# A two-layer hybrid trunk in one kernel: chunk inverses computed in pairs over four quadrants, SSD outputs and output tiles issued earlier

## The chip, the cores and the metric

One core of one Trainium2 chip. The metric is the device time of one execution in microseconds, the median of several runs.

## The reference, cut to what matters

Two layers over 384 tokens of 1024 features (128 of a context, 256 latent), in fp32. A layer does

```
h = rmsnorm(x) * (1 + scale) + shift
u = h @ w_in                       # attention 768, RWKV 896, SSD 772 columns
o = [attention | RWKV-7 | Mamba-2 SSD]      # 512 | 256 | 256 features
x = x + gate1 * (o @ w_out)
x = x + gate2 * moe(rmsnorm(x) ...)         # 16 experts, top 2 within the top group
```

RWKV-7 is a delta-rule scan in both directions: per step `S = S*w - (S kk) b' + v k'`, `y = S r`. In the kernel it is computed by chunks of 64 tokens, in which the delta rule is the inverse of a unit triangular 64x64 matrix `I - N` for each of 4 heads, each chunk and both directions.

## The kernel before, in words

All engines run hand-ordered instruction streams; semaphores tie them. Activations are kept transposed (feature by token, W = 385 columns with a gap between context and latent tokens). PSUM's eight banks are given out in turn by a plan (`psum_plan`, L225): the n-th group of matmuls takes bank n mod 8 and waits until the reader of group n - 8 (VectorE "v" or ScalarE "a") has read it (`open_bank`, L722). Weights come as items of 1 MB through SP's DMA queue, strictly in the order of their use (`homes_of`, L431); each item has a home, one of 5 ring slots, 3 places in `u`, 5 in the arena, one in `sq`, one in `hT`. From attention to the fourth output tile only two ring slots (`KEPT`) serve the stream; the others are lent as work space. Between the parts stand "fills": a twelfth of the next layers' modulation vectors, 2 items each (`fill`, L1076).

A layer runs: norm, input projection, attention, then the recurrence stage (`RW_ORDER`, from `rw_order`, L153), then `mixer_ends` (L1440), `out_projection` (L1485), norm, MoE.

The recurrence stage. Six batches (`RW_BATCHES`: a tile of two chunks in one direction; the two chunks stand on partitions 0-63 and 64-127) are inverted in three pairs (0,1), (2,3), (4,5). Each of the ten `RW_STEPS` is done for the first batch, then for the second, followed by SSD work (`SSD_BESIDE`) and, in the second and third pair, by the chunk recurrences whose inverses are done (values, carry, solve, state, output). On TensorE (`inverse_step`, L1280) "matrices" makes the products g4 and the base N (nd); "power1" to "power4" square N and its transpose (p) and build up the inverse of the 16x16 diagonal blocks (t: `inv += P^T' inv`); "transpose" gives `invT`; "cross0", "merge0", "cross1", "merge1" join the blocks to 32 and 64. A group `eight` (L1227) is 4 heads by two halves:

```
for j in range(4):
    for q in HALVES:
        last = mm(bank[q, at + 64 * j:at + 64 * j + 64], lhsT[q, j, :], rhs[q, j, :])
```

so rows 0-63 of the array feed columns 0-63, rows 64-127 feed columns 64-127. ScalarE (L1907) copies p, tT; VectorE (L2357) masks g4, nd, cross and adds t, t5, tt in place to `inv` or `invT`.

`mixer_ends`: RWKV's group mean (gnm), SSD's output of token tile 0 (`ssd_output`, L1461), the group variance (gnv), the fill "ssd", SSD's tiles 1 and 2, the fill "gate", and the mean square of the gated SSD output (yms), from which ScalarE and VectorE make features 6 and 7 of `o`. `out_projection` makes x's 8 feature tiles n for the tokens 0 to 256 (half 0), then for the rest. `OUT_AHEAD` = 2 tiles begin with features 0 to 5 (attention and RWKV) and get 6 and 7 when `mix_ready` is up. The weight items of tiles 0-1 and 2-3 take the two ring slots after the gate's, those of 4-5 and 6-7 further ring slots.

GpSimd (L938) issues DMAs only: cache and state outputs, row scatters and gathers of the MoE.

Of the kernel before, what the change touches and what calls it, by code (L numbers as in the profile page):

```python
# [13 lines left out]
P = 128  # L14
D = 1024
KT = D // P
TILES = 3
# [90 lines left out]
RW_STEPS = ["matrices", "power1", "power2", "power3", "power4", "transpose", "cross0", "merge0", "cross1", "merge1"]  # L108
# [19 lines left out]
def recurrence(q):  # L128
# [9 lines left out]
SSD_BESIDE = {  # L138
    (0, "matrices"): [("ssd_columns", 0), ("ssd_rows", 0)],
    (0, "power1"): [("ssd_rows", 1)], (0, "power2"): [("ssd_rows", 2)],  # L140
    (0, "power3"): [("ssd_rows", 3)], (0, "power4"): [("ssd_carry", 0)],
    (0, "transpose"): [("ssd_tokens", 0)], (0, "cross0"): [("fill", "rw"), ("ssd_tokens", 1)], (0, "merge0"): [("ssd_tokens", 2)],
    (0, "cross1"): [("ssd_args", 0)], (0, "merge1"): [("ssd_args", 1)],
    (2, "matrices"): [("ssd_args", 2)], (2, "power1"): [("ssd_args", 3)],
    (2, "power2"): [("ssd_decays", 0), ("ssd_args", 4)], (2, "power3"): [("ssd_args", 5)],
    (2, "power4"): [("ssd_args", 6)], (2, "transpose"): [("ssd_args", 7)], (2, "cross0"): [("ssd_decays", 1)],
    (2, "merge0"): [("ssd_queries", 0)], (2, "cross1"): [("ssd_queries", 1)], (2, "merge1"): [("ssd_queries", 2)],
    (4, "matrices"): [("fill", "rw2"), ("ssd_queries", 3)], (4, "power1"): [("ssd_values", 0)], (4, "power2"): [("ssd_values", 1)],
    (4, "power3"): [("ssd_values", 2)], (4, "transpose"): [("ssd_scores", 0)], (4, "cross0"): [("ssd_scores", 1)],
    (4, "merge0"): [("ssd_scores", 2)]}  # L150
# [64 lines left out]
OUT_AHEAD, SSD_FEATURES = 2, 6  # L215
# [9 lines left out]
def psum_plan():  # L225
# [11 lines left out]
    for l in range(DEPTH):  # L237
# [44 lines left out]
        for step, b in RW_ORDER:  # L282
            if step == "matrices":
                for half in range(2):
                    g("v", "g4", l, b, half)
                for half in range(2):
                    g("v", "nd", l, b, half)
            elif step[:5] == "power":
                k = int(step[-1])
                if k > 1:  # L290
                    g("v", "t", l, b, k)
                if k < 4:
                    g("a", "p", l, b, k)
            elif step == "transpose":
                g("a", "tT", l, b)
            elif step[:5] == "cross":
                g("v", "cross", l, b, int(step[-1]))
            elif step == "merge0":
                g("v", "t", l, b, 5)
                g("v", "tt", l, b, 0)  # L300
            elif step == "merge1":
                g("v", "tt", l, b, 1)
            elif step == "factors":
# [28 lines left out]
            elif step == "ssd_states":  # L332
                g("v", "hst", l)
        for i in range(2):
            g("v", "gnm", l, i)
        for grp in range(2):
            g("v", "ys", l, 0, grp)
# [3 lines left out]
        for t in range(1, TILES):  # L341
            for grp in range(2):
                g("v", "ys", l, t, grp)
# [87 lines left out]
def homes_of(stream, plan):  # L431
# [6 lines left out]
    for n, (where, _) in enumerate(stream):  # L438
# [63 lines left out]
def program(nc, a):  # L502
# [6 lines left out]
    with ctx:  # L509
# [221 lines left out]

        def filled(eng, *key):
# [70 lines left out]
        state_ready = sem("state_ready")  # L803
        matrices_ready = sem("matrices_ready")
        gn_in_ready = sem("gn_in_ready")
# [63 lines left out]
        def _(sp):  # L869
            sp.dma_start(cond[:, :], a["cond"][:, :]).then_inc(cond_loaded, 16)  # L870

            def home_free(l, n):

                name, i = HOMES[home[n]]
                if item_before[n] is not None:
# [62 lines left out]
        def _(pool):  # L938
# [80 lines left out]
        def _(pe):  # L1019
# [206 lines left out]

            def eight(bank, at, lhsT, rhs):  # L1227
# [6 lines left out]
            def rwkv_step(l, step, b):  # L1234
                if step == "fill":
                    fill(l, b)
                elif step in RW_STEPS:
# [42 lines left out]
            def inverse_step(l, step, b):  # L1280
                t, d = RW_BATCHES[b]
                s = b % 2
                pw, pwT = power[s][:, 0, :, :], power[s][:, 1, :, :]
                if step == "matrices":
                    if b == 0:
                        pe.wait_ge(factors_ready, 2 * l + 2)
                    banks_ = [open_bank(pe, "g4", l, b, half) for half in range(2)]
                    for i in range(2):
                        for k in range(2):
                            for c, q in enumerate(HALVES):  # L1290
                                c0 = COL[t] + CHUNK * c
                                for half, p in enumerate(HALVES):
                                    at = (2 * i + k) * P
                                    last = mm(banks_[half][q, at:at + P], kb[p, k, d, i, c0:c0 + CHUNK],
                                              ar[p, d, i, :, c0:c0 + CHUNK])
                                    if i and k and c:
                                        last.then_inc(psum_filled, 1)
                    banks_ = [open_bank(pe, "nd", l, b, half) for half in range(2)]
                    for i in range(2):
                        for c, q in enumerate(HALVES):  # L1300
                            c0 = COL[t] + CHUNK * c
                            for half, p in enumerate(HALVES):
                                last = mm(banks_[half][q, i * 64:i * 64 + 64], ar[p, d, i, 0, c0:c0 + CHUNK],
                                          kb[p, 1, d, i, c0:c0 + CHUNK])
                                if i and c:
                                    last.then_inc(psum_filled, 1)
                elif step[:5] == "power":

                    k = int(step[-1])
                    if k == 1:  # L1310

                        pe.wait_ge(matrices_ready, len(RW_BATCHES) * l + b + 1)
                    else:
                        bank = open_bank(pe, "t", l, b, k)
                        taken(pe, "p", l, b, k - 1)
                        if k > 2:
                            taken(pe, "t", l, b, k - 1)
                        eight(bank, 0, pwT, inv[s]).then_inc(psum_filled, 1)
                    if k < 4:
                        bank = open_bank(pe, "p", l, b, k)  # L1320
                        last = eight(bank, 256, pw, pwT)
                        if k < 3:
                            last = eight(bank, 0, pwT, pw)
                        last.then_inc(psum_filled, 1)
                elif step == "transpose":
                    bank = open_bank(pe, "tT", l, b)
                    taken(pe, "t", l, b, 4)
                    for j in range(4):
                        for q in HALVES:
                            last = mm(bank[q, 64 * j:64 * j + 64], inv[s][q, j, :], C("ident64", q))  # L1330
                    last.then_inc(psum_filled, 1)
                elif step[:5] == "cross":

                    k = int(step[-1])
                    bank = open_bank(pe, "cross", l, b, k)
                    if k:
                        taken(pe, "t", l, b, 5)
                    eight(bank, 0, g4[b][:, :, 2, :], inv[s]).then_inc(psum_filled, 1)
                elif step[:5] == "merge":
                    k = int(step[-1])  # L1340
                    if k == 0:
                        bank = open_bank(pe, "t", l, b, 5)
                        taken(pe, "cross", l, b, 0)
                        taken(pe, "tT", l, b)
                        eight(bank, 0, invT[b], cross[s]).then_inc(psum_filled, 1)
                    bank = open_bank(pe, "tt", l, b, k)
                    taken(pe, "cross", l, b, k)
                    if k:
                        taken(pe, "tt", l, b, 0)
                    eight(bank, 0, cross[s], invT[b]).then_inc(psum_filled, 1)  # L1350

            def recurrence_step(l, step, q):
# [17 lines left out]
                if step == "values":  # L1370
                    bank = open_bank(pe, "rv", l, q)
                    taken(pe, "tt", l, batches[1], 1)
# [19 lines left out]
                elif step == "solve":  # L1392
                    bank = open_bank(pe, "x", l, q)
                    taken(pe, "rv", l, q)
# [45 lines left out]
            def mixer_ends(l):  # L1440

                for i in range(2):
# [3 lines left out]
                ssd_output(l, 0)  # L1446
# [5 lines left out]
                ssd_output(l, 1)  # L1452
                ssd_output(l, 2)
                fill(l, "gate")
                bank = open_bank(pe, "yms", l)
                pe.wait_ge(gated_sq_ready, l + 1)
                for i in range(2):
                    last = mm(bank[:, 0:W], C("ones"), sq[:, 2 + i, :], i == 0, i == 1)
                last.then_inc(psum_filled, 1)
# [35 lines left out]

# [1490 lines left out]
```

## Time and profile before

| | us |
|---|---|
| median of 3 runs (1082.76 to 1089.31) | 1085.03 |
| profiled execution, its own time | 1091.34 |
| its span | 1089.5 |
| TensorE busy, share of the span | 969.5, 89% |
| VectorE / ScalarE busy | 483.1 / 275.3 |
| mean granted TensorE clock | 0.967 |

The profile is of one execution. Busy time of TensorE contains pipelining: a matmul's record runs on while the next has begun. fp32 matmuls are two instructions each. Weight loads have records of their own (PEld). All matmuls come from the helper at L1035, so a group is told by its operands: the inversions are `sb_u` with `sb_u`, `sb_tmp`, `sb_arena` or `sb_consts`, products and bases `sb_hT` with `sb_sq`, the output projection `sb_o` with `sb_ring`. A clock of 1.0 is 2.4 GHz, 0.5 is 1.2 GHz.

### The profile page before, as it was taken

How to read it: one execution, taken by the hardware profiler on the slowest of the kernel's cores; microseconds unless marked ns; L12 is line 12 of the kernel's file. 1: busy time of each engine (PE TensorE's matmuls, PEld its weight loads, DVE VectorE, ACT ScalarE, POOL GpSimd, SP SyncE). 2: the span in 40 equal slices, each digit the busy share in tenths (PEclk: the TensorE clock that was granted, in tenths of full speed). 3: DMA queues.
4: the chain of work that ended last, by engine and by line, in shares of the span. 5: the costliest groups of instructions: out<-in, count | busy, mean ns of one | idle time of the engine just before them, and what ended most of it. 6: DMA issues, size and time to landing. Idle time of an engine off the chain costs nothing. (4 is left out here: it accounts for less than half of the span.)

```text
span 1089.5 us, 25653 instructions
## 1 busy us (share of the span) xinstructions
PE 969.5 (89%) x11169; PEld 703.1 (65%) x11169; DVE 483.1 (44%) x1373; ACT 275.3 (25%) x628; POOL 51.4 (5%) x79
## 2 busy tenths in 40 slices
PE   6799998988879989978999998999987998996596
PEld 4455566778758875645845555778866977663265
DVE  1362388567732433113456066747853351311125
ACT  2330317332111601210242123643210241111000
POOL 0000000000000020012000000000000002001120
PEclk9899999999989999989999999999998999999899
DMA  9769633422268779999732204332038649999992
GB/s 382 290 159 273 160 106 127 157 81 86 82 247 343 301 226 399 373 359 406 312 118 78 78 5 155 118 118 81 9 122 338 263 173 329 375 360 356 374 387 60
DMA packets 43448, 238.75 MB, mean 219 GB/s; under 512 B 5120, under 2 KB 8192, under 8 KB 19904
## 3 DMA queue, kind: packets, MB, share of 16 engines
q1 hardware_dynamic: 29904, 196.37, 47.0%
q0 software_dynamic: 9584, 34.35, 10.5%
q10 hardware_dynamic: 3840, 6.29, 1.8%
q8 instruction: 93, 1.52, 0.6%
q14 instruction: 27, 0.22, 0.1%
HBM read 210.25 MB, written 26.74 MB: 218 GB/s over the span
## 5 line engine op out<-in xcount | busy, mean ns | idle before, releaser
L1035 PE MATMUL bank<-sb_hT,sb_ring 128*128 128x385 f32 (+1 forms) x640 | 208.3, 495 | 4.4 <-ACT sb_hT L1714 4.4
L1035 PEld LDWEIGHTS bank<-sb_hT,sb_ring 128*128 128x128 f32 (+1 forms) x640 | 116.7, 188 | 91.2 <-issue 11.8
L1035 PE MATMUL bank<-sb_arena 64*64 64x64 f32 (+5 forms) x1048 | 102.3, 334 | 8.5 <-DVE sb_arena L2651 3.0
L1035 PE MATMUL bank<-sb_ring,sb_arena 128*64 128x256 f32 (+4 forms) x672 | 91.5, 401 | 18.1 <-PEq L1668 10.9
L1714 ACT ACTIVATE sb_u<-bank 128x256 f32<-128x256 f32 (+4 forms) x106 | 48.7, 476 | 210.9 <-PE bank L1035 201.8
L1035 PE MATMUL bank<-sb_o,sb_ring 128*128 128x257 f32 (+1 forms) x512 | 88.2, 335 | 4.5 <-DMA sb_ring<-weights 4.5
L1035 PEld LDWEIGHTS bank<-sb_o,sb_ring 128*128 128x128 f32 x512 | 79.8, 195 | 14.7 <-issue 3.3
L1035 PEld LDWEIGHTS bank<-sb_ring,sb_arena 128*64 128x64 f32 (+2 forms) x672 | 57.0, 153 | 45.9 <-issue 29.9
L1035 PEld LDWEIGHTS bank<-sb_arena 128*64 128x64 f32 (+2 forms) x1048 | 58.2, 141 | 35.5 <-issue 21.9
L2074 DVE SCALAR_TENSOR_TENSOR sb_xT<-bank,sb_mod,sb_xT 128x128 f32<-128x128 f32 x144 | 41.1, 345 | 85.1 <-PE bank L1035 84.9
L1035 PE MATMUL bank<-sb_u,sb_arena 64*64 64x64 f32 (+2 forms) x744 | 63.1, 316 | 13.4 <-ACT sb_arena L1714 5.9
L1035 PE MATMUL bank<-sb_ring,sb_scond 128*32 128x128 f32 x1536 | 51.5, 287 | 22.5 <-DMA sb_ring<-weights 22.1
L1035 PE MATMUL bank<-sb_u 64*64 64x64 f32 x1592 | 54.5, 221 | 8.5 <-DVE sb_u L2071 6.2
L1035 PEld LDWEIGHTS bank<-sb_ring,sb_scond 128*32 128x32 f32 x1536 | 42.8, 115 | 28.4 <-DMA sb_ring<-weights 15.0
L1714 ACT ACTIVATE sb_tmp<-bank 128x128 f32<-128x128 f32 (+2 forms) x39 | 10.8, 276 | 197.1 <-PE bank L1035 185.6
L1714 ACT ACTIVATE sb_arena<-bank 128x512 f32<-128x512 f32 (+4 forms) x65 | 34.2, 539 | 103.4 <-PE bank L1038 32.6
L1035 PEld LDWEIGHTS bank<-sb_u 64*64 64x64 f32 x1592 | 49.9, 136 | 15.0 <-DVE sb_u L2071 8.7
L1035 PEld LDWEIGHTS bank<-sb_u,sb_arena 64*64 64x64 f32 (+1 forms) x744 | 38.5, 138 | 30.0 <-issue 13.5
L2767 DVE COPY sb_u<-bank 128x385 f32<-128x385 f32 x20 | 11.1, 557 | 99.7 <-PE bank L1035 99.7
L1035 PE MATMUL bank<-sb_u,sb_o 64*128 64x128 f32 (+2 forms) x672 | 49.8, 270 | 2.6 <-DVE sb_u L2074 2.1
L1035 PEld LDWEIGHTS bank<-sb_u,sb_o 64*128 64x128 f32 (+2 forms) x672 | 46.4, 181 | 7.4 <-DVE sb_u L2074 3.3
L1035 PE MATMUL bank<-sb_sq,sb_consts 128*128 128x385 f32 (+3 forms) x180 | 43.4, 391 | 1.4 <-DVE sb_sq L2071 1.4
(220 smaller groups left out, 1219.2 us busy)
## 6 DMA issues: line engine op xcount, KB each, us to landing
sb_ring<-weights SPq DMA_DIRECT2D x110, 1024.0 KB, 11.6
sb_arena<-weights SPq DMA_DIRECT2D x37, 1024.0 KB, 20.1
sb_u<-weights SPq DMA_DIRECT2D x18, 1024.0 KB, 12.5
sb_sq<-weights SPq DMA_DIRECT2D x8, 1024.0 KB
sb_hT<-weights SPq DMA_DIRECT2D x8, 1024.0 KB
x_slots<-sb_o POOLq DMA_DIRECT2D x1, 6912.0 KB, 39.9
sb_sq<-x_slots POOLq DMA_DIRECT2D x18, 256.0 KB, 7.8
sb_hT<-x_slots POOLq DMA_DIRECT2D x17, 256.0 KB, 7.7
```

The lines of the kernel that those rows point to most:

```text
L1035: return nc.tensor.matmul(out, lhsT, rhs, start=start, stop=stop, skip_group_check=True)
L1714: return nc.scalar.activation(out, in_, func, **kw)
L2074: return v.scalar_tensor_tensor(out, x, s, y, op0, op1)
L2767: v.tensor_copy(u[:, tile, 1:W + 1], bank[:, 0:W]).then_inc(read("u", l, c), 1)
```

## The change

The inversion steps of a pair are issued as one. `sixteen` interleaves the two batches' groups; batch b keeps rows q to columns q, batch b + 1 crosses: the result of rows q goes to columns of the other half, so its matrices change halves with every product. In-place additions between halves can't be done, so the second batch gets them through the left factor (`cross[1]` = P^T + 1, or the power itself plus 1) and ScalarE copies its results; for cross terms GpSimd adds ones to `g4[:, :, 2, :]` and the masks get a diagonal, so all merges become copies. Products and bases of a pair are made beside the pair before. tt0 stays as two groups of eight. SSD's output of tile 0 moves ahead of the group mean, tile 1 ahead of the variance. Four output tiles begin, with features 0 to 3 (attention): two ahead of yms, two behind it; the first weight item of the out-projection gets the home in `hT` and waits for the last `yS`.

```
-RW_STEPS = ["matrices", "power1", ...
+RW_STEPS = ["power1", "power2", "power3", "power4", "transpose", "cross0", "merge0", "cross1", "merge1"]
...
+BESIDE = {
+    (0, "power1"): [("ssd_rows", 3), ("ssd_carry", 0)], (0, "power2"): [("products", 2)],
+    (0, "power3"): [("products", 3)], (0, "power4"): [("ssd_tokens", 0)], (0, "transpose"): [("ssd_tokens", 1)],
+    (0, "cross0"): [("fill", "rw"), ("ssd_tokens", 2)], (0, "merge0"): [("ssd_args", 0)],
+    (0, "cross1"): [("bases", 2), ("ssd_args", 1)], (0, "merge1"): [("ssd_args", 2)],
+    (2, "power1"): [("products", 4), ("ssd_args", 3)], (2, "power2"): [("products", 5), ("ssd_decays", 0)],
...
+    (4, "power1"): [("fill", "rw2"), ("ssd_queries", 3)], (4, "power2"): [("ssd_values", 0)],
...
-    out = []
+    out = [("products", 0), ("products", 1), ("bases", 0), ("ssd_columns", 0)] + [("ssd_rows", k) for k in range(3)]
...
-            out += [(step, first), (step, first + 1)] + SSD_BESIDE.get((first, step), [])
+            out += [(step, first)] + BESIDE.get((first, step), [])
...
-OUT_AHEAD, SSD_FEATURES = 2, 6
+OUT_AHEAD, RW_FEATURES, SSD_FEATURES = 4, 4, 6
...
+        elif kind == "fixed" and where[2] == MOD_ITEMS + IN_ITEMS:
+            i = HOMES.index(("hT", 0))
...
# GpSimd
+                for b in range(len(RW_BATCHES)):
+                    pool.wait_ge(powers_ready, len(RW_BATCHES) * l + b - b % 2 + 2)
+                    left = g4[b][:, :, 2, :]
+                    pool.tensor_tensor(left, left, bc(C("ident64"), 1, 4), ALU.add).then_inc(cross_left_ready, 1)
# TensorE
+            def sixteen(banks_, at, lhsT, rhs, turned=(0, 1)):
+                for j in range(4):
+                    last = []
+                    for m in range(2):
+                        for i, q in enumerate(HALVES):
+                            out = HALVES[(i + turned[m]) % 2]
+                            ins = mm(banks_[m][out, at + 64 * j:at + 64 * j + 64], lhsT[m][q, j, :], rhs[m][q, j, :])
+                        last.append(ins)
+                return last
...
+                    if k < 4:
+                        banks_ = [open_bank(pe, "p", l, m, k) for m in pair[::-1]]
+                        if k > 1:
+                            taken(pe, "p", l, b, k - 1)
+                        last = sixteen(banks_, 256, pw[::-1], pwT[::-1], (1, 0))
+                        if k < 3:
+                            last = sixteen(banks_, 0, pwT[::-1], pw[::-1], (1, 0))
...
+                    if k > 1:
+                        banks_ = [open_bank(pe, "t", l, m, k) for m in pair]
...
+                        for ins in sixteen(banks_, 0, [pwT[0], pwT[1] if k == 4 else cross[1]], inv):
...
+                    for m in range(2):
+                        eight(banks_[m], 0, cross[m], invT[pair[m]]).then_inc(psum_filled, 1)
...
             def mixer_ends(l):
+                ssd_output(l, 0)
                 for i in range(2):
                     bank = open_bank(pe, "gnm", l, i)
...
-                ssd_output(l, 0)
+                ssd_output(l, 1)
...
                 fill(l, "ssd")
-                ssd_output(l, 1)
                 ssd_output(l, 2)
                 fill(l, "gate")
...
+                taken(pe, "pv", l, 2)
+                for n in (0, 1):
+                    attention_features(n)
+                bank = open_bank(pe, "yms", l)
...
+                for n in range(2, OUT_AHEAD):
+                    attention_features(n)
...
-                    add_features(bank, n, 0, range(SSD_FEATURES))
+                    add_features(bank, n, 0, range(RW_FEATURES, SSD_FEATURES))
# ScalarE
+                        for m in (1, 0):
+                            if k == 2 and m == 0:
+                                filled(act, "t", l, b, 2)
+                            elif k == 2:
+                                act.wait_ge(powers_plus_one, len(RW_BATCHES) * l + b + 1)
+                            copy(power[m].rearrange("p k j n -> p (k j) n"), "p", l, b + m, k)
+                    if k > 1:
+                        copy(inv[1], "t", l, b + 1, k)
# VectorE
+                elif step == "bases":
...
+                    for s, m in enumerate(pair):
+                        tt(power[s][:, 1, :, :], g4[m][:, :, 2, :], bc(C("inv")[:, 0:64], 1, 4), ALU.mult)\
+                            .then_inc(powers_ready, 1)
...
+                    for i, q in enumerate(HALVES):
+                        last = tt(inv[1][HALVES[1 - i]], power[1][q, 0, :, :], bc(C("ident64", q), 1, 4), ALU.add)
...
+                        tt(cross[1], power[1][:, 1, :, :], one, ALU.add).then_inc(powers_plus_one, 1)
+                    if k == 3:
...
+                        tt(power[1][:, 1, :, :], four(bank, 256), one, ALU.add).then_inc(read("p", l, b + 1, 3), 1)
```

## Rows read from the trace of the kernel before

**Rows 1.** Stretches: length, busy us (instructions) by engine, granted clock, DMA share, GB/s
```profile
200.80:295.20 94.40, 83.73 (x2610) 75.79 (x2608) 66.10 (x217) 29.89 (x61) 1.08 (x2) 1.00 0.21 75
714.40:805.20 90.80, 81.45 (x2553) 73.57 (x2549) 66.00 (x217) 29.62 (x60) 1.08 (x2) 1.00 0.16 55
229.00:253.00 24.00, 21.82 (x780) 21.13 (x777) 20.61 (x67) 8.96 (x16) 0.00 (x0) 1.00 0.02 5
295.50:318.90 23.40, 15.59 (x228) 10.13 (x223) 11.35 (x28) 3.67 (x7) 0.00 (x0) 0.85 0.59 227
380.00:390.00 10.00, 8.99 (x49) 6.37 (x48) 7.28 (x37) 0.00 (x0) 2.24 (x3) 1.00 0.43 178
400.00:500.00 100.00, 91.26 (x703) 58.01 (x701) 20.34 (x50) 14.20 (x32) 9.11 (x16) 0.97 1.02 368
```

**Rows 2.** TensorE's waits from 200.8 to 295.2 us
```profile
PE bank L1035 <- issue: 5.0, 5, 2.2
```

**Rows 3.** Timeline (start, length, what): two-quadrant groups, then weight loads over four
```profile
222.88 0.63 PE L1035 MATMUL bank<-sb_u,sb_tmp 64*64 64x64 f32 x16
...
223.34 0.63 PE L1035 MATMUL bank<-sb_tmp,sb_u 64*64 64x64 f32 x16
...
201.61 0.38 PEld L1035 LDWEIGHTS bank<-sb_sq,sb_hT 64*64 64x64 f32 x16
...
201.90 0.87 PEld L1035 LDWEIGHTS bank<-sb_hT,sb_sq 64*64 64x64 f32 x32
```

**Rows 4.** VectorE's timeline, second and third output tile added to x
```profile
327.81 0.61 DVE L2074 SCALAR_TENSOR_TENSOR sb_xT<-bank,sb_mod,sb_xT 128x128 f32<-128x128 f32 x2 [0.26 <-PE bank L1035]
331.27 0.61 DVE L2074 SCALAR_TENSOR_TENSOR sb_xT<-bank,sb_mod,sb_xT 128x128 f32<-128x128 f32 x2 [2.86 <-PE bank L1035]
```

**Rows 5.** VectorE's timeline in the recurrence stage, layer 0
```profile
204.71 1.28 DVE L2071 TENSOR_TENSOR sb_arena<-bank,sb_consts 128x512 f32<-128x512 f32 x2
...
206.42 0.42 DVE L2071 TENSOR_TENSOR sb_u<-sb_arena,sb_consts 128x256 f32<-128x256 f32 x1
...
206.76 0.42 DVE L2071 TENSOR_TENSOR sb_u<-sb_u,sb_consts 128x256 f32<-128x256 f32 x1
...
245.45 0.87 DVE L2074 SCALAR_TENSOR_TENSOR sb_ring<-sb_ring,sb_u,sb_consts 128x128 f32<-128x128 f32 x3
```

**Rows 6.** ScalarE's timeline in the recurrence stage, layer 0
```profile
208.43 0.60 ACT L1714 ACTIVATE sb_u<-bank 128x512 f32<-128x512 f32 x1 [1.79 <-PE bank L1035]
...
216.81 1.92 ACT L1714 ACTIVATE sb_ring<-sb_ring 128x2048 f32<-128x2048 f32 x1
...
241.71 0.92 ACT L1714 ACTIVATE sb_u<-bank 128x256 f32<-128x256 f32 x3
```

**Rows 7.** TensorE's timeline: power1 of batches 0, 2, 4; the last merge
```profile
204.85 1.15 PE L1035 MATMUL bank<-sb_u 64*64 64x64 f32 x32
...
232.99 1.15 PE L1035 MATMUL bank<-sb_u 64*64 64x64 f32 x32 [0.45 <-DVE sb_u L2071]
...
259.66 2.08 PE L1035 MATMUL bank<-sb_u 64*64 64x64 f32 x64
...
281.15 0.97 PE L1035 MATMUL bank<-sb_u,sb_tmp 64*64 64x64 f32 x26 [0.24 <-DVE sb_tmp L2071]
```

**Rows 8.** TensorE's timeline from the ssd fill's end to the out-projection
```profile
303.36 1.10 PE L1035 MATMUL bank<-sb_ring,sb_arena 128*64 128x128 f32 x16
...
308.21 1.08 PE L1035 MATMUL bank<-sb_ring,sb_scond 128*32 128x128 f32 x32 [1.28 <-DMA sb_ring<-weights]
...
312.11 1.93 PE L1035 MATMUL bank<-sb_ring,sb_scond 128*32 128x128 f32 x32 [2.82 <-DMA sb_ring<-weights]
...
313.97 2.94 PE L1035 MATMUL bank<-sb_sq,sb_consts 128*128 128x385 f32 x4
...
318.91 11.46 PE L1035 MATMUL bank<-sb_o,sb_ring 128*128 128x257 f32 x44 [2.00 <-DMA sb_ring<-weights]
```

**Rows 9.** One microsecond of the out-projection, columns as in rows 1
```profile
321.00:322.00 1.00, 1.00 (x3) 0.73 (x3) 0.00 (x0) 0.00 (x0) 0.00 (x0) 0.50 0.86 319
```

More of the change, by code:

```diff
@@ L134, in recurrence @@
     return out[:-2] + out[-1:] if q == CHUNKS - 1 else out
[L138 to L150, printed above, removed]
+BESIDE = {
[4 more added lines that the diff above has]
+    (2, "power1"): [("products", 4), ("ssd_args", 3)], (2, "power2"): [("products", 5), ("ssd_decays", 0)],
+    (2, "power3"): [("ssd_args", 4)], (2, "power4"): [("ssd_args", 5)], (2, "transpose"): [("ssd_args", 6)],
+    (2, "cross0"): [("ssd_args", 7)], (2, "merge0"): [("ssd_decays", 1), ("ssd_queries", 0)],
+    (2, "cross1"): [("bases", 4), ("ssd_queries", 1)], (2, "merge1"): [("ssd_queries", 2)],
+    (4, "power1"): [("fill", "rw2"), ("ssd_queries", 3)], (4, "power2"): [("ssd_values", 0)],
+    (4, "power3"): [("ssd_values", 1)], (4, "power4"): [("ssd_values", 2)], (4, "transpose"): [("ssd_scores", 0)],
+    (4, "cross0"): [("ssd_scores", 1)], (4, "merge0"): [("ssd_scores", 2)]}
@@ L333, in psum_plan @@
                 g("v", "hst", l)
+        for grp in range(2):
+            g("v", "ys", l, 0, grp)
         for i in range(2):
@@ L336, in psum_plan @@
         for grp in range(2):
[L337 removed]
+            g("v", "ys", l, 1, grp)
         for i in range(2):
@@ L1236, in rwkv_step @@
                     fill(l, b)
-                elif step in RW_STEPS:
+                elif step in RW_STEPS or step in ("products", "bases"):
                     inverse_step(l, step, b)
@@ L1278, in ssd_step, with products @@
                     last.then_inc(psum_filled, 1)
-            def inverse_step(l, step, b):
+            def products(l, b):
                 t, d = RW_BATCHES[b]
[L1282 to L1299, printed above, removed]
+                banks_ = [open_bank(pe, "g4", l, b, half) for half in range(2)]
+                for i in range(2):
+                    for k in range(2):
                         for c, q in enumerate(HALVES):
@@ L1310, in inverse_step @@
                     if k == 1:
[L1312 to L1315, printed above, removed]
-                        if k > 2:
[L1317 to L1324, printed above, removed]
-                elif step == "transpose":
[L1326 to L1331, printed above, removed]
+                        pe.wait_ge(powers_ready, len(RW_BATCHES) * l + b + 2)
@@ L1332, in inverse_step @@
                 elif step[:5] == "cross":
                     k = int(step[-1])
-                    bank = open_bank(pe, "cross", l, b, k)
+                    banks_ = [open_bank(pe, "cross", l, m, k) for m in pair]
                     if k:
[L1337 to L1350, printed above, removed]
+                        for m in pair:
+                            taken(pe, "t", l, m, 5)
+                    else:
+                        pe.wait_ge(cross_left_ready, len(RW_BATCHES) * l + b + 2)
@@ L1371, in recurrence_step @@
                     bank = open_bank(pe, "rv", l, q)
-                    taken(pe, "tt", l, batches[1], 1)
+                    for d in range(2):
+                        taken(pe, "g4", l, batches[d], 1)
                     for j in range(4):
@@ L1393, in recurrence_step @@
                     bank = open_bank(pe, "x", l, q)
+                    for d in range(2):
+                        taken(pe, "tt", l, batches[d], 1)
                     taken(pe, "rv", l, q)
@@ L2377, in inverse_step @@
-                    tt(inv[s], power[s][:, 0, :, :], bc(C("ident64"), 1, 4), ALU.add).then_inc(matrices_ready, 1)
+                elif step == "bases":
+                    if b:
+                        taken(dve, "t", l, b - 2, 4)
+                        filled(dve, "t", l, b - 1, 4)
+                    for s, m in enumerate(pair):
+                        for half in range(2):
+                            bank = filled(dve, "nd", l, m, half)
+                            tt(power[s][:, 0, half::2, :], shaped(bank[:, 0:P], 2, 64),
+                               bc(C(f"nd{RW_BATCHES[m][1]}"), 1, 2), ALU.mult).then_inc(read("nd", l, m, half), 1)
+                    taken(dve, "g4", l, b + 1, 1)
+                    for s, m in enumerate(pair):
+                        tt(power[s][:, 1, :, :], g4[m][:, :, 2, :], bc(C("inv")[:, 0:64], 1, 4), ALU.mult)\
+                            .then_inc(powers_ready, 1)
+                    if b:
+                        filled(dve, "cross", l, b - 1, 1)
+                    taken(dve, "nd", l, b + 1, 1)
+                    tt(inv[0], power[0][:, 0, :, :], one, ALU.add).then_inc(matrices_ready, 1)
+                    for i, q in enumerate(HALVES):
+                        last = tt(inv[1][HALVES[1 - i]], power[1][q, 0, :, :], bc(C("ident64", q), 1, 4), ALU.add)
+                    last.then_inc(matrices_ready, 1)
```

200 lines of the change are left out of this document (140 added, 60 removed).

## The prediction

> **What bounds the kernel now.** I read the table of busy time by stretch first. Of the 1089.5 us span, 94.4 us in layer 0 and 90.8 us in layer 1 go to the recurrence stage (the inversions, the chunk recurrences, the SSD work beside them). There TensorE has 83.7 and 81.5 us of records, VectorE 66 us, and the DMA engines a fifth of their time [rows 1]: TensorE and what makes it wait. Of the 10.7 us without a record in layer 0, 5.0 are put down to "issue" [rows 2]: stretches in which matmul records are missing, since the counts there don't come out. So 5.7 us are waits, mostly for VectorE. The following 23.4 us (norms, SSD's outputs, gate) have 15.6 us of TensorE at a mean clock of 0.85 [rows 1]. In the MoE stage the DMA share is 1.02 from 400 to 500 us, but between 380 and 390 it is 0.43 [rows 1]: the weight homes are full and the queue waits, so that stage starts when TensorE arrives. What is won before the out-projection's end moves everything behind by as much, once in each layer.
>
> **The inversions.** A batch has 14 groups of 8 matmuls (16 instructions each, fp32 in two): two for each of power1 and power2, one for power3, and one each for t2, t3, t4, transpose, cross0, t5, tt0, cross1, tt1. Such a group takes 0.46 us start to start, 29 ns an instruction [rows 3]; it uses two quadrants (rows 0-63 to columns 0-63, 64-127 to 64-127). The "nd" group, 16 instructions of the same shape over all four quadrants, takes 0.29 us, 18 ns, by the two weight-load rows of [rows 3]. So a paired group of 32 instructions should take 0.52 to 0.58 us where two groups took 0.93. Per pair of batches 13 groups are paired (tt0 stays as two groups), 39 in a layer: 39 x (0.93 - 0.55) = 14.8 us, 16 at 16 ns. Can a pair keep that rate? The nd group sends each row half to its own PSUM bank, the paired group sends both to one. The old group of 8 does this too. An out-projection instruction streams 257 columns, and a tile of 16 of them takes 3.46 us [rows 4], 0.84 ns a column, so 64 columns are 54 ns in one quadrant: 29 ns is two quadrants at full overlap, and 18 ns nearly four.
>
> The Trainium skill (TensorEngine Tiling (Array Packing), "Gotcha 1: PSUM Pressure") says that different row tiles cannot use the same PSUM bank at once. By it the pairs would not overlap, and the gain of 14.8 us would be a loss (last rival). The 29 ns of today's group, which does just that, speak against it.
>
> **The round trips.** Before, while one batch's result was copied, TensorE had the other's matmuls; now it has only what stands beside. I followed pair 0 in layer 0: VectorE 0.60 us for a 128x512 mask, 0.34 for 128x256 start to start (0.42 alone) [rows 5]; ScalarE 0.60 for 512 columns, some 0.5 where two follow each other, and 0.92 for three of 256 [rows 6]; 0.2 us of matmul tail before a reader. Both power1 groups can start when the four masks and six small operations are through, about 206.5 us, against 204.85 for batch 0 alone [rows 7]. Then: power1 (1.1 us), copies of 0.6 + 0.5, the last of "ssd_rows" (0.85) hiding most; "ssd_carry", an exponential of 1.9 us [rows 6] moved up from power4, now stands ahead of power2's copies and costs some 1.4; power2 and t2 1.7 and copies 1.2, with "products" (0.82) under them; power3 to t4 5 us with a mask of 1.2 us in VectorE's way; transpose to merge1 about 8, 2.1 of it the modulation fill. Pair 2's power1 starts at 225.5, against 232.99 [rows 7]: its masks have been made beside pair 0.
>
> Pair 2 is bound by VectorE, whose queue I added up from its power1 to pair 4's: 4 masks 2.4, five "ssd_args" of three operations 4.0 (the last of [rows 5]), ten inversion operations of the powers, merges and 1+P^T terms with four crosses 4.4, bases (nine operations of some 0.3) 2.7, queries 2.1, two recurrence steps 3.8: 19.4 us, against 16 of TensorE. Pair 4's power1 is then at 244.9, against 259.66. Pair 4 has 18 us of TensorE (the fill, scores, two recurrence steps) and 17 of VectorE, with the round trips 21.2; before its last merge it took 21.5. So that merge comes at 266.1, against 281.15 [rows 7], and VectorE, whose backlog there is 1.2 us shorter, is 16.3 us ahead. My hand walk leaves out some 50 engine hand-overs of 20 to 40 ns: I take **15 us a layer**. The ends: 12 (the rate at 18 ns, and the waits grown by 3) and 20 (14.8 and nearly all 5.7 us of waits gone).
>
> ScalarE gets six copies of 256 columns a pair (18 x 0.38 = 7 us a layer, the 0.38 being the last of the three in [rows 6]) on 29.9 us [rows 1]: hidden, except in the order above. Its stalls for "ssd_decays" arguments are in the walk. VectorE loses three additions a pair and gains one.
>
> **GpSimd's ones.** No row shows such an operation. It is 128x256 with two SBUF inputs, six in a layer. VectorE does that shape in 0.42 us [rows 5], and cross0 needs it some 10 us after the powers are ready, so anything up to 5 us each is hidden: 0. Queued behind it on GpSimd are only the state outputs and later the row scatters, far behind. A loss is possible only if it stops VectorE: bounds 0 and its own time doubled, 6 x 0.84 = 5 us a layer. I take 0, as VectorE reads PSUM in the neighbouring steps.
>
> The Trainium skill (SBUF — State Buffer, "SBUF: two separate sides") has just such a lock between GpSimd and a VectorE operation with two SBUF inputs; GPSIMD Engine Reference ("Elementwise — side-by-side cycle accounting") gives 4.5 us for 2048 elements, from which I estimate 0.6 us for 256. By it the two additions would meet the inverses' first sums, 1.2 us a pair, 3.5 us a layer. No row here shows it.
>
> **The outputs moved up and the norm.** ssd_output(0) moves into a short wait ahead of the mean, output(1) into one ahead of the variance. The fill "ssd" starts no earlier by that: output(1), 1.3 us longer than output(0), now stands in front of it and takes what the two waits gave. The gate's two weight items are issued when that fill is done (303.36) and are used at 308.21 and 312.11, with waits of 1.28 and 2.82 us [rows 8]. That distance of 8.7 us stays, and output(1) no longer fills it. So gate's end moves by 0.25 us only.
>
> **Out-projection begun early.** Before, TensorE ends the gate at 313.97, does the sum of squares (2.9 us at half clock), and waits 2.00 us for its first weight item to 318.91 [rows 8]; then the clock falls again to 0.5 [rows 9], so the first two tiles are read at 327.81 [rows 4], 8.9 us later, in place of 6.9. After, this item goes to hT, free at the recurrence's end, and is loaded right behind the gate's two. At 2.6 us an item it should be there at 314.5. Attention features of two tiles: 16 instructions, half of them at the low clock, to 319.1; squares 1.5, to 320.6; two more tiles (their item comes at 318.9 as before) to 324.0. ScalarE's root and VectorE's scaling have 6.9 us from the squares until TensorE needs them at 327.5: hidden. RWKV's and SSD's features of four tiles, 32 x 0.217, to 330.9. Before, four tiles are done at 318.9 + 8.9 + 6.9 = 334.7. That is **3.9 us a layer** with the 0.25; ends 0 (the item late) and 6. The later items wait for the mixer's end as before and are needed at 331: hidden.
>
> **Sum.** 2 x (15 + 3.9) = 37.8 us off 1091.3, the profiled execution's own time, 1053.5. It lies 6.3 us above the median, so against 1085.0 I give **1047**.
>
> **Rivals.** (1) The round trips are less covered: the pairs' rate holds, but three hand-overs a pair fall behind VectorE masks or ScalarE exponentials as at power2 above, 3 x 3 x 0.9 = 8 us a layer. For it: VectorE is at 20.6 of 24 us between 229 and 253 [rows 1]. Against: masks are placed early. 2 x (7 + 3.9) = 22 less: 1063. (2) The opposite: every wait is covered, 2 x (20 + 6) = 52 less: 1033. Against: pair 0 has little beside. (3) GpSimd's lock, 3.5 us a layer: 1054. (4) The early item does nothing, because its load lands behind the gate's: 2 x 15: 1055. (5) Slower: two row halves in one bank with crossed columns exclude each other, each instruction takes its 54 ns: a paired group 1.71 us for 0.93, 39 x 0.78 = 30 us a layer, less some 8 for the waits and the rest: 1085 + 45 = 1130. It decides from 32 ns an instruction on. Against it: 18 and 29 ns.
>
> **Chances.** Forecast 0.55, (1) 0.2, (2) 0.06, (3) 0.05, (4) 0.08, (5) 0.06. The range 1032 to 1066 holds all but (5) and the worst of (1). Faster by over 1% (what a measurement of this kernel can tell from no change) 0.9, within 1% 0.04, slower 0.06.
>
> **What would show it.** Paired groups of 32 instructions at 16 to 18 ns in TensorE's timeline; the stage at 79 us for 94 and at 76 for 91; waits of TensorE there near 8 us, mostly for VectorE in pair 2; 28 us from the ssd fill's end to the fourth out tile ready instead of 31; half-clock still before the squares but not after them. I am wrong if paired instructions stand 25 ns or more apart, if TensorE waits over 12 us in the stage, or if the first out tile starts later than 2 us after the gate.

## The result, and the profile after

| | before | after |
|---|---|---|
| median (runs) | 1086.28 us (6) | 1077.07 us (6, 1071.88 to 1078.08) |
| ratio, 95% interval | 1 | 0.9907 (0.9878 to 0.9936) |
| span of the profiled execution | 1089.5 | 1075.4 |
| recurrence stage, layer 0 / layer 1 | 94.8 / 90.9 | 97.5 / 92.0 |
| end of the stage to the fourth output tile, layer 0 / layer 1 | 39.1 / 38.8 | 35.3 / 35.2 |

The kernel is 9 us faster where 38 were forecast. The stage (from its first g4 product to the end of the last yS) was to be 15 us shorter in each layer. In these two traces it is not shorter at all. TensorE's busy time in it did fall, by 10 to 12 us; the windows of the two stages, columns as in [rows 1]:

```profile
199.60:297.10 97.50, 73.16 (x2620) 63.95 (x2616) 67.01 (x213) 33.99 (x76) 6.23 (x8) 0.93 0.21 74
709.80:801.80 92.00, 69.50 (x2555) 60.69 (x2553) 66.58 (x211) 33.73 (x75) 6.24 (x8) 0.96 0.15 54
```

The granted clock is 0.93 and 0.96 where it was 1.00 in both stages before [rows 1]: some 13.6 us of layer 0's stage and 6.8 of layer 1's ran at half clock, in three and two stretches. Three of the five, without their edges:

```profile
227.00:233.00 6.00, 4.54 (x89) 4.21 (x89) 3.47 (x11) 1.09 (x3) 0.00 (x0) 0.50 0.03 7
271.00:274.00 3.00, 2.79 (x89) 2.79 (x90) 2.07 (x9) 0.38 (x1) 0.00 (x0) 0.50 0.02 5
742.00:745.00 3.00, 2.96 (x45) 2.63 (x46) 0.81 (x3) 1.08 (x2) 0.00 (x0) 0.50 0.03 5
```

That can have cost half of it at most, 6.8 and 3.4 us (an estimate from these rows).

What was won as busy time came back as waits. TensorE's waits in layer 0's stage (who was waited for: us in all, times, longest), against the 5.0 of [rows 2]:

```profile
PE bank L1061 <- issue: 11.7, 7, 3.6
PE bank L1061 <- ACT sb_u L1792: 5.1, 7, 1.4
PE bank L1061 <- DVE sb_tmp L2168: 2.7, 4, 0.9
PE bank L1061 <- DVE sb_u L2168: 2.1, 3, 0.8
PE bank L1061 <- DVE sb_state_rw L2171: 1.7, 1, 1.7
```

The largest is "issue", in which the profile shows no engine and no transfer that TensorE waited for. TensorE's timeline at the second pair's power1 shows what it is:

```profile
225.26 0.45 PE L1061 MATMUL bank<-sb_u 64*64 64x64 f32 x13 [0.61 <-DVE sb_u L2168]
228.46 1.65 PE L1061 MATMUL bank<-sb_u 64*64 64x64 f32 x50 [2.75 <-issue]
...
229.90 0.31 PE L1061 MATMUL bank<-sb_u 64*64 64x64 f32 x1
```

A power1 of a pair has 64 matmuls, and 13 + 50 + 1 are there: no record is missing. TensorE stood still in the middle of one group of 32, and the kernel has its waits only ahead of a group. Such holes come regularly (242.01, 246.14, 249.81, 253.41). Ahead of the first three, one small burst is on the DMA engines some 2 us before matmuls resume, and hardly anything beside it. The windows of a quarter of a microsecond, and the 4 us from one burst to the next:

```profile
239.50:239.75 0.25, 0.25 (x32) 0.25 (x26) 0.15 (x1) 0.15 (x1) 0.00 (x0) 1.00 0.23 66
243.75:244.00 0.25, 0.25 (x23) 0.25 (x21) 0.25 (x2) 0.25 (x2) 0.00 (x0) 1.00 0.23 66
247.50:247.75 0.25, 0.25 (x16) 0.25 (x13) 0.21 (x2) 0.04 (x1) 0.00 (x0) 1.00 0.23 66
...
239.75:243.75 4.00, 2.64 (x129) 2.29 (x120) 3.83 (x16) 1.03 (x4) 0.00 (x0) 1.00 0.01 2
```

66 GB/s for 0.25 us are 16.5 KB. The page's table of DMA queues has a queue with packets of just that size:

```profile
q8 instruction: 92, 1.51, 0.6%
```

1.51 MB in 92 packets are 16.4 KB each. The program has 11169 matmuls and as many weight loads, so a packet holds 121 matmuls with their loads on average, beside whatever else it carries; 129 matmuls ran between two bursts here, and the probe below runs exactly 128 at a time. In these holes a packet comes every 3.6 to 4.1 us: 28 to 32 ns a matmul, however fast the quadrants are. That is what the expectations below call theory S: the supply of instructions bounds the stage. Their theory R is that it doesn't, and that only TensorE's rate and the round trips through VectorE and ScalarE count. The limit had hidden in [rows 3], since two quadrants take 29 ns a matmul, nearly the same figure.

The output part is shorter by what was forecast, 3.8 us in layer 0 and 3.6 in layer 1. VectorE's timeline of the output tiles, the fourth of them at 332.39 where the stage ended at 297.1:

```profile
329.78 0.61 DVE L2171 SCALAR_TENSOR_TENSOR sb_xT<-bank,sb_mod,sb_xT 128x128 f32<-128x128 f32 x2 [5.23 <-PE bank L1061]
...
332.39 0.61 DVE L2171 SCALAR_TENSOR_TENSOR sb_xT<-bank,sb_mod,sb_xT 128x128 f32<-128x128 f32 x2 [0.26 <-PE bank L1061]
```

### The profile page after: what moved, and what is told of

It reads as the page before. It is cut to its first block and busy times, and to the rows that moved or that the text cites. A ratio compares the mean times of both kernels' runs of the same rounds, so it can differ in the third digit from the quotient of the medians.

```text
span 1075.4 us, 25701 instructions
## 1 busy us (share of the span) xinstructions
PE 942.4 (88%) x11169; PEld 675.1 (63%) x11169; DVE 484.5 (45%) x1361; ACT 283.5 (26%) x658; POOL 62.0 (6%) x91
## 3 DMA queue, kind: packets, MB, share of 16 engines
q8 instruction: 92, 1.51, 0.6%
## 5 line engine op out<-in xcount | busy, mean ns | idle before, releaser
L1061 PEld LDWEIGHTS bank<-sb_hT,sb_ring 128*128 128x128 f32 (+1 forms) x640 | 116.4, 188 | 90.9 <-issue 11.1
L1792 ACT ACTIVATE sb_u<-bank 128x256 f32<-128x256 f32 (+4 forms) x136 | 57.9, 456 | 240.6 <-PE bank L1061 230.1
L1061 PE MATMUL bank<-sb_ring,sb_arena 128*64 128x256 f32 (+4 forms) x672 | 91.5, 402 | 14.1 <-PEq L1746 10.4
L1061 PE MATMUL bank<-sb_ring,sb_scond 128*32 128x128 f32 x1536 | 53.9, 295 | 22.2 <-DMA sb_ring<-weights 21.7
L1061 PE MATMUL bank<-sb_u,sb_arena 64*64 64x64 f32 (+2 forms) x744 | 59.0, 323 | 12.8 <-ACT sb_arena L1792 5.9
L1061 PE MATMUL bank<-sb_o,sb_ring 128*128 128x257 f32 (+1 forms) x384 | 64.4, 327 | 0.0
L1061 PEld LDWEIGHTS bank<-sb_o,sb_ring 128*128 128x128 f32 x384 | 58.0, 190 | 5.9
L1061 PE MATMUL bank<-sb_u 64*64 64x64 f32 x1400 | 36.7, 232 | 22.1 <-issue 7.9
L1061 PEld LDWEIGHTS bank<-sb_u,sb_arena 64*64 64x64 f32 (+1 forms) x744 | 34.1, 140 | 28.5 <-issue 16.0
L1061 PEld LDWEIGHTS bank<-sb_u 64*64 64x64 f32 x1400 | 31.6, 143 | 28.1 <-issue 15.4
L1061 PE MATMUL bank<-sb_sq,sb_consts 128*128 128x385 f32 (+3 forms) x180 | 40.8, 375 | 0.2
```

The costliest lines, as they stand in the source:

```text
L1061: return nc.tensor.matmul(out, lhsT, rhs, start=start, stop=stop, skip_group_check=True)
L1792: return nc.scalar.activation(out, in_, func, **kw)
```

## The experiments

Stage lengths below are measured alike, layer 0 / layer 1, each from one trace. Times are set against the kernel before as it was measured together with the run, 1088.44 us for e1 to e4.

**e1_groups_apart**: in the kernel after, each batch's group by itself.

```
-                for j in range(4):
-                    last = []
-                    for m in range(2):
+                last = []
+                for m in range(2):
+                    for j in range(4):
...
-                        last.append(ins)
+                    last.append(ins)
```

> The kernel after, but sixteen issues batch b's 8 matmuls and then batch b+1's (29 ns an instruction, two quadrants at a time) in place of interleaving them; everything else, also the number of instructions, is the same. Theory S (TensorE runs out of instructions: in the traces a packet burst of some 16 KB comes every 3.6 to 3.8 us while it stalls for 'issue', which is 128 matmuls with their weight loads, 28 ns each): the stalls for issue shrink by nearly what the groups grow, time 1077 to 1085. Theory R (round trips to ScalarE and VectorE, TensorE's rate counts in full): 39 groups x 0.4 us x 2 layers = 31 us more, 1108.

Measured: 1075.65 us, ratio to before 0.990 (0.9864 to 0.9935), stages 94.8 / 90.9. The 64 matmuls of power1 take 1.50 us start to start (205.92 to 207.42), 23 ns each in place of 17. They are slower, but less so than the 29 ns expected; presumably one group's end overlaps the next one's crossed quadrants. In layer 0 TensorE's busy time grew from 73.2 to 77.4 us, and the issue waits fell from 11.7 to 8.3. The time is that of the kernel after, within some 4 us, so the rate of the paired groups is worth nothing that can be measured. The clock changed too: layer 0's stage ran at 1.00 throughout in place of 0.93, so its 2.7 us less than after can be the clock's. It is still no shorter than before. The half clock alone therefore doesn't explain the missing gain.

**e2_outputs_only**: the kernel before with the output parts alone (the order in mixer_ends, four tiles begun, the item in hT).

> The kernel before with only the output parts of the change (SSD outputs moved up, four output tiles begun early, the first item's home in hT). Both theories: the gain of the term as predicted, 3.9 us a layer, 1086 to 1078. If so, the inversions give nothing at all. If this run stays at 1086, the 9 us measured come from the inversions.

Measured: 1082.29 us, 0.9948 (0.9921 to 0.9974), 5.6 us less than before; from the stage's end to the fourth tile 35.0 us for 39.1. That is 4.1 us in layer 0 and 3.2 in layer 1 (38.8 to 35.6), and 5.6 in all is seen in the time; the interval reaches from 2.8 to 8.6. Layer 1's stage, which this edit leaves alone, is 92.6 us for 90.9: a stage's length from one trace can't tell differences of under 2 us.

**e3_inversions_only**: the kernel after without the output parts.

> The kernel after without the output parts. Theory S with the trace's stage lengths (97.5 and 92.0 us for 94.8 and 90.9): 1084 to 1089, no gain against before. Theory R says the same, my prediction said 1056.

Measured: 1082.9 us, 0.9959 (0.9933 to 0.9985), stages 97.6 / 90.2. The inversions, forecast at 30 us, bring 4.5 (1.6 to 7.3), and with e2's 5.6 they make up the 9 to 10 of the whole change. The stretch to the fourth tile is 37.4 / 37.0 here, 1.7 and 1.8 shorter than before without any output part. In layer 0 the second stretch at half clock, which before has in the out-projection [rows 9], is missing in e3. So part of the 3.8 us in the two traces comes without the output parts, and beside the new inversions these parts bring 2.1 and 1.8.

**p4_four_quadrants** and **p2_two_quadrants**: in the kernel before, ahead of one cross group of the second pair, 512 fp32 products (1024 matmul instructions) of constants that nothing waits for, once over four quadrants, as shown (rows i to columns o), and once over two, with (0, 0), (1, 1) twice.

```
+                    if (l, b, k) == (0, 2, 1):
...
+                        for n in range(128):
+                            c = 64 * (n % 4)
+                            for to, i, o in ((0, 0, 0), (0, 1, 1), (1, 0, 1), (1, 1, 0)):
+                                last = mm((bank, banks[after % 8])[to][HALVES[o], c:c + 64],
+                                          C("ident64", HALVES[i]), C("ident64", HALVES[i]))
```

> The kernel before with a probe: in layer 0, between 240 and 255 us, TensorE does 512 more 64x64 matmuls (1024 instructions with as many weight loads) on constants, over all four quadrants, into two banks. Nothing waits in between and the DMA engines are idle there. Theory S: it starts at 16 to 18 ns an instruction, runs dry after some 128 to 300 instructions, and then shows stalls of 1 to 2 us every 128 instructions, 3.6 us apart: 28 to 30 us in all. Theory R: 1024 x 17 ns = 17.4 us without a stall.

> The same probe with the same instructions over two quadrants only. Theory S and theory R: 1024 x 29 ns = 29.7 us with hardly a stall, so as long as the four-quadrant probe by S, 12 us longer by R.

TensorE's timeline, four quadrants:

```profile
255.43 2.09 PE L1036 MATMUL bank<-sb_consts 64*64 64x64 f32 x128 [1.49 <-issue]
259.16 2.09 PE L1036 MATMUL bank<-sb_consts 64*64 64x64 f32 x128 [1.64 <-issue]
262.63 2.10 PE L1036 MATMUL bank<-sb_consts 64*64 64x64 f32 x128 [1.37 <-issue]
266.36 2.09 PE L1036 MATMUL bank<-sb_consts 64*64 64x64 f32 x128 [1.64 <-issue]
```

and two quadrants:

```profile
246.84 30.64 PE L1036 MATMUL bank<-sb_consts 64*64 64x64 f32 x1024
```

Four quadrants run exactly 128 matmuls in 2.1 us, 16 ns each, and stand still until the next 128, every 3.5 to 3.7 us here and up to 4.0 in the rest of the probe. The whole took from 252.04 to 283.0, 31 us or 30 ns a matmul; two quadrants take 30.6 without a hole. Nothing in the probe waits for data, a semaphore or another engine, and its length is the same. This is theory S by itself. The clock doesn't make the holes, for it was 1.00 through the first seven of them and fell only then:

```profile
252.00:278.00 26.00, 14.50 (x888) 13.54 (x882) 1.13 (x4) 0.38 (x1) 0.00 (x0) 1.00 0.02 4
279.00:285.00 6.00, 5.13 (x152) 4.75 (x149) 0.42 (x1) 0.00 (x0) 0.00 (x0) 0.50 0.02 5
```

The whole times, 1123.48 and 1110.55 us, are single runs; of the 13 us between them 5.2 lie ahead of the probe, and they say nothing of it.

**e4_no_ones**: GpSimd's additions left out (a nop raises the semaphore); the cross terms lack their ones, so the numbers behind differ.

> The kernel after with GpSimd's six additions of ones in each layer left out (the output is not the reference's), its semaphore kept. Theory G (GpSimd's 0.85 us operation holds up VectorE: the three sums behind it take 2.15 us in place of 1.1): 1 us at each of six places, and the copies of power1 come 1 us earlier, 1071. Theory S: that wait is mostly hidden behind the wait for instructions, 1075 to 1077.

Measured: 1067.22 us, 0.981 (0.9758 to 0.9862). But the stages are 95.7 / 92.4, 1.8 shorter and 0.4 longer than after, both too little for single traces. Of the 9.4 us that the span is shorter, 6.9 lie behind layer 1's stage, and the trace has 49 fewer matmuls in all (11120 for 11169), presumably because the routed part follows the data. This run can't price the lock.

**e5_ones_by_vector**: the same additions by VectorE, behind the inverses' first sums; the result is whole.

```
-                    pool.tensor_tensor(left, left, bc(C("ident64"), 1, 4), ALU.add).then_inc(cross_left_ready, 1)
...
+                    for m in pair:
+                        left = g4[m][:, :, 2, :]
+                        tt(left, left, one, ALU.add).then_inc(cross_left_ready, 1)
```

> The kernel after with the ones added by VectorE, right behind the inverses' first sums, in place of GpSimd. Six operations of 0.34 us a layer more on VectorE, without the 1 us hold-up at each pair. Theory G: 3 x (1.0 - 0.7) = 1 us a layer better, 1075. Theory S: 1076 to 1078.

Measured: 1078.23 us, 0.9898 (0.9861 to 0.9935), stages 97.0 / 90.2. The timelines of GpSimd and VectorE in the kernel after:

```profile
225.28 1.70 POOL L976 TENSOR_TENSOR sb_arena<-sb_arena,sb_consts 128x256 f32<-128x256 f32 x2 [18.41 <-DVE sb_u L2168]
...
225.12 2.15 DVE L2168 TENSOR_TENSOR sb_u<-sb_u,sb_consts 128x256 f32<-128x256 f32 x3
```

and VectorE's here, without GpSimd beside it:

```profile
224.97 1.31 DVE L2164 TENSOR_TENSOR sb_u<-sb_u,sb_consts 128x256 f32<-128x256 f32 x3
```

An addition takes GpSimd 0.85 us beside VectorE (no run has it alone), and VectorE's three operations take 2.15 in place of 1.31. So GpSimd does hold VectorE up, by 0.84 us a pair in layer 0, 2.5 a layer. The time is the same all the same. VectorE's own two additions take 0.76 us of the 0.84 back:

```profile
226.31 0.76 DVE L2164 TENSOR_TENSOR sb_arena<-sb_arena,sb_consts 128x256 f32<-128x256 f32 x2
```

Only the inverses' first sums come earlier. So this run can't price the lock in the kernel's time either.

**e7_two_heads_each** and **e8_before_two_heads**: a matmul streams two heads with the first one's weights, in the kernel after and in the kernel before.

```
-                for j in range(4):
+                for j in (0, 2):
...
-                            ins = mm(banks_[m][out, at + 64 * j:at + 64 * j + 64], lhsT[m][q, j, :], rhs[m][q, j, :])
+                            ins = mm(banks_[m][out, at + 64 * j:at + 64 * j + 128], lhsT[m][q, j, :], rhs[m][q, j:j + 2, :])
```

> The kernel after, but each matmul of a paired group streams two heads (128 columns) with the weights of the first, and the loads and matmuls of the second are left out; what the second head's half should be is not computed. A paired group is 16 instructions for 32, with the same columns streamed; 39 groups a layer, 624 of some 2610 matmuls of the stage gone. Theory S (instructions come at about 28 ns a matmul): most of 624 x 0.028 = 17 us a layer go until the waits for VectorE and ScalarE take over; layer 0's stage, 97.5 us in the kernel after, ends between 80 and 88 us, with 'issue' waits under 4 us (11.7 before this edit), and power1 of the third pair begins 8 to 10 us after less than 22 us of pair 1 (30.4 now). Rival H (the round trips through VectorE and ScalarE set the stage, the issue waits only fill them): a paired group shortens by 0.1 us, 39 x 0.1 = 4 us at most, stage 93 to 97 us. Only the stage's length counts, as the routed work behind it changes with the data.

> The kernel before with the edit of e7_two_heads_each: each matmul of a group of eight streams two heads (128 columns) with the weights of the first, the second's are left out. Same columns through two quadrants, half the instructions. Theory S+A (before, the supply of 28 ns a matmul and the two quadrants, 29 ns for 64 columns, bound alike; halving the instructions lifts only the first): a group stays at 0.43 to 0.46 us and layer 0's stage at 91 to 95 us (94.8 before), so that the four quadrants are worth 4 to 8 us in e7 (86.9) once the instructions come fast enough. Rival F: if fewer instructions alone do it and the quadrants nothing, the stage falls to 86 to 88 us as in e7.

| stage, us | all instructions | half in the groups |
|---|---|---|
| two quadrants (before, e8) | 94.8 / 90.9 | 91.7 / 88.4 |
| four quadrants (after, e7) | 97.5 / 92.0 | 86.9 / 84.6 |

In e7 layer 0's stage loses 10.6 us with the same columns streamed, and its issue waits are gone (11.7 to 0.8). What is left of TensorE's waits there:

```profile
PE bank L1061 <- ACT sb_u L1792: 6.2, 9, 1.4
PE bank L1061 <- DVE sb_tmp L2168: 5.9, 6, 1.7
PE bank L1061 <- DVE sb_u L2168: 2.8, 4, 0.8
PE bank L1061 <- DVE sb_state_rw L2171: 2.8, 1, 2.8
PE bank L1061 <- issue: 0.8, 1, 0.8
```

Rival H, 93 to 97 us, is out. Part of the 10.6 can be the clock's, which is 0.98 here for 0.93: at most 5.1 us, an estimate from 3.4 us at half clock for 13.6. The issue waits alone fell by 10.9. But the second pair took 25.3 us from its power1 (226.22) to the third's (251.47), not the under 22 that I expected: the round trips come up as soon as the supply is out of the way. e8 keeps 55 ns a matmul of 128 columns (groups at 224.30 and 224.73, 0.43 us for 8) and 91.7 us: with few instructions the two quadrants bound it. So fewer instructions alone give 3.1 and 2.5 us, the paired inversions alone lose 2.7 and 1.1, and both together give 7.9 in layer 0 and 6.3 in layer 1. Two things blur this table. The lower line has the whole new order, with ScalarE's copies and GpSimd's ones, not only the quadrants. And the clock differs: e8 has 0.96 in layer 0, which can hide up to 3.5 us of its gain there (estimate: half of 7 us at half clock), but 1.00 in layer 1, where e7 is 3.8 us shorter although its own clock is 0.98. The whole times, 1059.84 and 1080.6, are single runs with other data, and not to be compared.

**e6_apart_by_vector**: e1 and e5 together, the result whole.

> The kernel after with the order of e1_groups_apart (each batch's group by itself, two quadrants) and the ones by VectorE as in e5_ones_by_vector, with the whole result computed. Theory S: as each edit alone left the time at 1075.65 and 1078.23, both together give 1072 to 1078, the same as the kernel after; stage of layer 0 94 to 96 us. Rival: if the order apart has left VectorE's additions and GpSimd's lock as the next bound, taking the lock away there gives its 3 us a layer: 1068 to 1071.

Measured: 1072.05 us (1068.34 to 1074.26), 0.9886 (0.9852 to 0.9921) to a before of 1084.54; stages 94.8 / 89.9 at a clock of 1.00 and 0.98, issue waits 9.0 us in layer 0. It is the fastest whole kernel here, but its interval overlaps that of the kernel after, so whether it beats that one stays open. The median lies at the edge of theory S's range and 1 us above the rival's, which it doesn't rule out.

## Why the prediction was wrong

**"Stretches in which matmul records are missing"** is the step that failed. [Rows 2] stood there: 5.0 us of "issue" in five pieces. I explained them away because counts seemed not to come out, and did not count the instructions of one step on both sides of a hole. Before, at the second merge of pair 0:

```profile
226.11 0.70 PE L1035 MATMUL bank<-sb_u,sb_tmp 64*64 64x64 f32 x17
228.62 0.56 PE L1035 MATMUL bank<-sb_u,sb_tmp 64*64 64x64 f32 x12 [1.80 <-issue]
...
229.01 0.22 PE L1035 MATMUL bank<-sb_u,sb_tmp 64*64 64x64 f32 x2
...
229.07 0.22 PE L1035 MATMUL bank<-sb_u,sb_tmp 64*64 64x64 f32 x1
```

17 + 12 + 2 + 1 are the 32 of the two groups: nothing is missing here. They were stalls of the supply, by what p4 shows of such holes. From them, and from the table of DMA queues, the limit of 28 ns a matmul could have been worked out. The second pair's stretch alone would have shown it: before, 843 matmuls in 26.7 us (233 to 259.7), 32 ns each, 13% above that limit. A walk that let this pair pass in 19.4 us asked for 25 ns each of the 777 matmuls that the pair's stretch has after. What the runs show in its place: 11.7 and 7.1 us of issue waits, a stage of 97.5 and 92.0 us for the 79 and 76 forecast, and 86.9 and 84.6 once the groups have half the instructions (e7).

**39 x (0.93 - 0.55) = 14.8 us.** The 0.55 was right: paired groups run at 16 to 18 ns. By the Trainium skill (TensorEngine Tiling (Array Packing), "Gotcha 1: PSUM Pressure") they would not have overlapped in one bank; rival 5 rested on it, and power1's 64 matmuls in 1.1 us rule it out for halves that go to different partitions. What failed is that the term stands only if the instructions come: in e1 and e3 it is worth nothing measurable in the stage. TensorE's busy time fell by 10.6 and 12.0 us, less than 14.8, with part of it spent at half clock.

**The hand walk.** It was right up to the first long hole: pair 2's power1 at 225.26, forecast 225.5. From there on it was wrong twice. The third pair's power1 came at 255.71, forecast 244.9. Of these 11 us some 5 are the supply's, with the half clock that came with it, for e7 takes 25.3 us for that pair in place of 30.5. The other 6 are there in e7 too: the sum of VectorE's 19.4 us was no bound by itself, and the round trips add to it (rival 1, which I had at 7 or 8 us a layer less gain). Over the whole stage the supply, with its half clock, cost more, 10.6 and 7.4 us by e7; with the round trips alone the stages would have gained 8 and 6 us of the 15.

**The clock.** The walk had no term for it in the stage. Half clock there can have cost up to 6.8 and 3.4 us, which are not to be added to the supply's cost, since the slower matmuls also fill time in which TensorE would have waited for instructions. In e1 and e6 layer 0's stage has no half clock and takes 94.8 us, as before.

**The outputs.** Forecast 3.9 us a layer; 3.8 and 3.6 between the two traces, 4.1 and 3.2 in e2; the time of e2 shows 5.6 of the 7.8. Rival 4 is out. The agreement is in part luck, as e3 has 1.7 and 1.8 of it without any output part.

**GpSimd's ones at 0**: no run shows them to cost time, but the reason was wrong. The lock that the Trainium skill describes (SBUF — State Buffer, "SBUF: two separate sides") is there, at 0.84 us a pair. My estimate for it was 1.2, which made rival 3's 3.5 us a layer; the trace has 2.5. That it costs nothing because the supply covers it was not shown: e4 has other data, and e5 only moves the additions.

**Waits.** I had said that I am wrong if TensorE waits over 12 us in the stage: it waits 24 us in layer 0. The other two marks stayed silent: paired instructions stand 17 ns apart, and the first output tile starts 0.6 us after the gate.

**What stays open.** Between the two profiled executions 10.6 of the 14.1 us lie behind layer 1's stage, 3.6 of them up to the fourth output tile and 6.9 behind it. That last stretch is 245.3 us before, 241.6 in e2, 238.4 in e3 and 238.4 after. It is 238.9 in p2, which there is the kernel before, so such a difference between two traces need not come from the change. In e3, which has no output parts, the stages are together 2.1 us longer than before, and yet it is 4.5 us faster. One difference there is a hole of 4.2 us <-issue on the chain that ended last, before:

```profile
1032.01 4.20 issue
```

With all its pieces TensorE's issue waits behind 800 us are 4.2 us before, 4.3 in e2, and 1.4 and 1.2 in the two kernels with paired inversions. An edit moves every instruction behind it within the packets, and with it where a hole falls against weight loads. That this is where the rest comes from was only argued; no run was made for it. So where the inversions' 4.5 us are won stays open.

## What to carry to other kernels

Count instructions as a resource: where small fp32 matmuls run one after another, compare their number in a stretch with what the instruction queue brings before you credit a faster rate. Take an "issue" wait in the middle of one group for a stall until its records have been counted. Two limits of the same size hide each other: here lifting one alone gave 3.1 us at best. Fewer and wider instructions with faster quadrants gave 7.9 and 6.3 us a stage, in a kernel whose result isn't whole; how to get there with the whole result was not tried.

## What the runs showed of the hardware that was not expected

- TensorE's instructions came in packets of about 128 matmuls with their loads (16.4 KB), every 3.5 to 4.1 us while TensorE waited for them: 30 ns a matmul over the 1024 of p4, 16 ns within a packet.
- The two longest holes come behind 1 MB weight loads: 2.75 us up to 228.46 (360 GB/s from 226 to 227) and 3.6 us up to 271.20 (410 GB/s from 266.5 to 267.6). That the loads held up the packet was not tried alone.
- The clock fell around stalls, but not at each: in the microsecond of the hole at 226 the granted clock was 0.72, and after the hole it was 0.5, 1.2 GHz; the stage's mean fell from 1.00 [rows 1] to 0.93. In p4 seven holes of 1.4 to 1.9 us passed at 1.00 before it fell to 0.5, and before, five issue waits of up to 2.2 us left it at 1.00.
- Beside VectorE, GpSimd takes 0.85 us for a 128x256 addition of two SBUF inputs, and holds up VectorE's operations of the same kind by 0.84 us a pair.
